# Block-sparse attention of an eight-core decoder kernel: finer filler, early masks added in PSUM, an early gate tile, blocks in another order, shorter waits of the exponentials

## Chip, cores, metric

One Trainium2 chip, all 8 cores, each with two of the 16 sequences and no exchange between them. The metric is device time in microseconds (us) of the slowest core, median of the runs.

## The reference, cut to what matters

```python
for l in range(2):                       # x (16, 2048, 1024)
    h = rms_norm(x, g_pre); proj = h @ w_in          # q/k/v of 16 heads, gate_a, gate_b
    o_a = dilated attention, 3 groups of 4 heads, combined by softmax denominators
    # block-sparse: each query sees its own block of 256 keys and the 3 best-gated past ones
    s = q @ k.T * SCALE - slope * dist; s = where(dist >= 0, s, -inf)    # 4 heads
    o_b = softmax(s) @ v
    merged = sigmoid(gate_a) * (o_a @ W_a) + sigmoid(gate_b) * (o_b @ W_b)
    x = x + rms_norm(merged @ w_out, g_post)
    h = rms_norm(x, g_pre2); u = gelu(conv3(h @ w_gate)) * (h @ w_up)
    x = x + rms_norm(u @ w_down, g_post2)
```

## The kernel before

A core runs four mixers (2 sequences x 2 layers), each followed by its feed-forward part. The normed, transposed activations `hT` (bf16, 8 chunks of 128 rows x 2048 tokens) stay in SBUF; weights come through a ring of 8 slabs, loaded by GpSimd's queue (`Stream`, L303). `Q` (L29) puts every engine's program in the order in which Python emits it, with semaphore waits; each engine is in order. The emission order is made by generators that yield costs in us: `merge(main, fill, ratio)` (L83) gives the filler `ratio` times the cost of what the main generator has yielded, `par` (L119) runs several side by side, `chain` one after the other.

A mixer has three parts:

- Six dilated units (`dil_unit`, L660), with projections of the next unit as filler (`proj_fm`, L621: four groups of eight 512-column products, 1.75 us each, for tokens 0-511, ...). GpSimd adds the units' results (L748) from `tz` buffers that ScalarE fills (L372).
- The block-sparse part (`moba`, L876). Its units are (block, kt, h): a block `(qg, pair)` is 512 queries of one pair of heads; kt runs over the 4*qg+4 tiles of 128 keys, h over the two heads: 160 units in the order of `blocks` (L877), of which 8 of each block touch the diagonal. Unit n issues the scores S (L943, up to 512 columns, into banks 0 to 2), the exponential on ScalarE into `Pm` (L951), on the diagonal a multiplication with the 0/1 triangle `tri` on VectorE (L955), and then, four units behind (`SKEW`), the product with V (L656) into bank 3 or 4. At a block's end VectorE copies both heads' sums out (L972), and a chain of small DMAs over DRAM takes their denominators to 128 partitions, where VectorE inverts them (L908), and back (`norm_den`, `norm_recip`, `bcast`), until `norm_mult` (L900) writes `obT`. `todo` starts these steps after counts of units, so that no queue should wait. The filler `fill_m` (L1113) runs, side by side, the last q projection followed by the top-3 selection of pair 1 (`gating`, L821: tiny products L837, MAX8 L848, transposes L866), the same selection of pair 0, and the denominators of the dilated heads (`dil_den`, L755, ends with four multiplications L785 of 64x1024); it then waits for the first four blocks to be `done` and goes on with the gates of the first 1024 tokens.
- `gates` (L983): per 128 output columns and 512 tokens two gate projections with Tanh (L1001, L1007) and two branch products (`wbr`) multiplied in on VectorE (L1013 to L1022); then `tail_out` (products L538) beside the gates of the other half.

The exponentials (L949) wait on `waits`, here `m_wait` (L1096), which holds the last GpSimd additions of the dilated units (`st["u_last"]`).

Of the kernel before, what the change touches and what calls it, by code (L numbers as in the profile page):

```python
# [8 lines left out]
BF16 = mybir.dt.bfloat16  # L9
AF = mybir.ActivationFunctionType  # L10
ALU = mybir.AluOpType
# [71 lines left out]
def merge(main, fill, ratio):  # L83
    credit = 0.0
    live = fill is not None
    for cost in main:
        credit += cost * ratio
        while live and credit > 0:
            try:
                credit -= next(fill)  # L90
            except StopIteration:
                live = False
    if live:
        for _ in fill:
            pass

# [39 lines left out]
def build(n_seq=2, n_layers=2):  # L136
# [16 lines left out]
    tri_d = dt_in("tri", [128, 128], BF16)  # L153
    qaug_d = dt_in("qaug_t", [4, 64, SEQ], BF16)
# [9 lines left out]
    with es:  # L164
# [24 lines left out]
        tri = sb("tri", [128, 128], BF16)  # L189
        pastc = sb("pastc", [128, 3, 128], F32)  # L190
# [381 lines left out]
        AB = [carve((12 + 2 * i) * KB, 512) for i in range(4)]  # L572
        uT = carve(0, 11264, BF16).rearrange("p (c t) -> p c t", c=NFC)
# [302 lines left out]
        def moba(qk_toks, aug_toks, sel_toks, vm_toks, done, waits, on_p0):  # L876
            blocks = [(0, 0), (1, 0), (0, 1), (1, 1), (2, 0), (2, 1), (3, 0), (3, 1)]  # L877
# [27 lines left out]
            def norm_recip(k, qg, pair, tl):  # L905
# [11 lines left out]
                todo.append([16 if k < 4 else 28, lambda: norm_mult(k, qg, pair, rt)])  # L917
                todo.append([6 if k < 4 else 10, bcast])

            def norm_den(k, qg, pair, te):  # L920
# [8 lines left out]
                todo.append([6 if k < 4 else 10, gather])  # L929
                todo.append([16 if k < 4 else 24, lambda: norm_recip(k, qg, pair, tl)])  # L930

            for n in range(len(units) + SKEW):
                if n < len(units):
# [9 lines left out]
                    tS = PE.do(nc.tensor.matmul(ps[bS][:, 0:nq], lhsT=Kx[:, kt * 128:(kt + 1) * 128],  # L943
                                                rhs=Qx[:, qg * 512 + c0:(qg + 1) * 512], start=True, stop=True))
# [4 lines left out]
                    ACT.wait(tS, pfree[sl], waits)  # L949
# [33 lines left out]
        def gates(l, hf, oa_toks, ob_done, banks, waits, toks, wload):  # L983
            abf = st.setdefault("ab_free", [[], [], [], []])
            mT = mTs[hf]
            for oc in range(8):
                bga, tga, sga = load_w(l, 24 + oc)
                bgb, tgb, sgb = load_w(l, 32 + oc)
                bwa, twa, swa = wbr_ring.load((l, oc, 0))
                bwm, twm, swm = wbr_ring.load((l, oc, 1))  # L990
                tp = None
                for tgi in range(2):
                    tg = 2 * hf + tgi
                    tsl = slice(tg * 512, (tg + 1) * 512)
                    ia = tgi * 2
                    A_, B_ = AB[ia], AB[ia + 1]
                    b_ga = banks.get()
                    t_ga = mm_group(ps[b_ga], [(bga[:, kc * 128:(kc + 1) * 128], hT[:, kc, tsl]) for kc in range(8)],
                                    [tga, hT_tok[4 * tg:4 * tg + 4]])
                    ACT.wait(t_ga, abf[ia], waits)  # L1000
                    s1 = ACT.do(nc.scalar.activation(out=A_, in_=ps[b_ga], func=AF.Tanh, scale=0.5))  # L1001
                    bank_free[b_ga] = [s1]
                    yield 1.75
                    b_gb = banks.get()
                    t_gb = mm_group(ps[b_gb], [(bgb[:, kc * 128:(kc + 1) * 128], hT[:, kc, tsl]) for kc in range(8)], [tgb])
                    ACT.wait(t_gb, abf[ia + 1])
                    s2 = ACT.do(nc.scalar.activation(out=B_, in_=ps[b_gb], func=AF.Tanh, scale=0.5))  # L1007
                    bank_free[b_gb] = [s2]
                    yield 1.75
                    b_ya = banks.get()  # L1010
                    t_ya = mm_group(ps[b_ya], [(bwa[:, kc * 128:(kc + 1) * 128], oaT[:, kc, tsl]) for kc in range(2)], [twa, oa_toks])
                    DVE.wait(s1, t_ya)
                    m1 = DVE.do(nc.vector.scalar_tensor_tensor(out=A_, in0=A_, scalar=1.0, in1=ps[b_ya], op0=ALU.add, op1=ALU.mult))  # L1013
                    bank_free[b_ya] = [m1]
                    b_yb = banks.get()
                    t_yb = mm_group(ps[b_yb], [(bwm[:, kc * 128:(kc + 1) * 128], obT[:, kc, tsl]) for kc in range(2)], [twm, ob_done(tg)])
                    tp = t_yb
                    DVE.wait(s2, t_yb)
                    m2 = DVE.do(nc.vector.scalar_tensor_tensor(out=B_, in0=B_, scalar=1.0, in1=ps[b_yb], op0=ALU.add, op1=ALU.mult))
                    bank_free[b_yb] = [m2]  # L1020
                    DVE.wait(m1, m2, waits)
                    m3 = DVE.do(nc.vector.tensor_tensor(out=mT[:, oc, tgi * 512:(tgi + 1) * 512], in0=A_, in1=B_, op=ALU.add))  # L1022
                    abf[ia] = [m3]
                    abf[ia + 1] = [m3]
                    toks.append(m3)
                    wload()
                    yield 0.9
                slab_ring.release(sga, tp)
                slab_ring.release(sgb, tp)
                wbr_ring.release(swa, tp)  # L1030
                wbr_ring.release(swm, tp)
# [5 lines left out]
        def mixer(s, l, xs_tok, p_wait, pre):  # L1037
# [15 lines left out]
            for i, (g, sp) in enumerate(order):  # L1053
# [36 lines left out]
                merge(dil_unit(g, sp, QK[i % 2], qt[(g, sp)], vt[g], acc_free, res), fill, max(total, 20.0 if i == 3 else 0.0) / 6.9)  # L1090
# [22 lines left out]
            def fill_m():  # L1113
                yield from par(chain(mqk_proj(l, 1, 0, w1, mq[1], FB2), gating(1, mq[1], aug_t[1], sel[1], FB2)),
                               gating(0, mq[0], aug_t[0], sel[0], FB2), dil_den(1, m_wait, nt1))
                while not all((q, p) in done for q in range(2) for p in range(2)):
                    yield 0.5
                yield from gates(l, 0, nt1, ob_done, FB2, nt1, mts, wout_load)
            merge(moba(mq, aug_t, sel, vt[3], done, m_wait, on_p0), fill_m(), 1.25)
# [323 lines left out]
```

How the kernel before makes its waits and increments, by code:

```python
    def wait(self, *toks):  # L49
        acc = {}
        self._collect(toks, acc)
        for so, v in acc.items():
            if self.seen.get(so, 0) >= v:
                continue
            self.seen[so] = v
            if self.pending is not None:
                self.eng.wait_ge(self.pending[0].sem, self.pending[1])
                self.pending = None
            if self.attach:
                self.pending = (so, v)
            else:
                self.eng.wait_ge(so.sem, v)
# [1 line left out]
    def flush(self):  # L64
        if self.pending is not None:
            self.eng.wait_ge(self.pending[0].sem, self.pending[1])
            self.pending = None
# [1 line left out]
    def do(self, inst):  # L69
        if self.pending is not None:
            inst._wait_ge(self.pending[0].sem, self.pending[1])
            self.pending = None
        inst.then_inc(self.so.sem, 1)
        self.so.n += 1
        return (self.so, self.so.n)
# [98 lines left out]
        def dma_tr(out, in_, so):  # L174
            nc.sync.dma_start_transpose(out=out, in_=in_).then_inc(so.sem, 16)
            so.n += 16
            return (so, so.n)
# [1 line left out]
        def dma(q, out, in_, so, **kw):  # L179
            q.eng.dma_start(out=out, in_=in_, **kw).then_inc(so.sem, 16)
            so.n += 16
            return (so, so.n)
```

## Time and profile before

| | |
|---|---|
| median of 3 runs | 3836.77 us (3836.76 to 4285.7) |
| profiled execution, own time | 3838.05 us |
| its span (first to last instruction, slowest core) | 3836.7 us |
| spans of the 8 cores | 3830.6 to 3836.7 us |
| block-sparse parts (first to last S) | from 257 to 387, 1198 to 1331, 2142 to 2273, 3088 to 3220 us |

The time and the span of the profiled execution lie 1.35 us apart. "Busy" adds up instructions; a wait is put down to what released it last. A TensorE row is drawn with its whole latency: the next product may start before it ends.

### The profile page before, as it was taken

To read this page: it belongs to the slowest core of one execution; us is meant where nothing else is said; L and a number is where in the kernel's file an instruction comes from. 1 tells how busy PE (TensorE), PEld (TensorE's weight loads), DVE (VectorE), ACT (ScalarE), POOL (GpSimd) and SP (SyncE) were. 2 spreads that over 40 slices of the span, in tenths; PEclk is the share of its full clock that TensorE was granted. 3 is DMA by queue.
4 is the path that set the end of the run, shared out by engine and by line. 5 is a ranking of instruction groups with operands and counts; after the bars stand their busy time and mean duration, and the time that the engine had idled before them with its cause. 6 is when DMAs were issued, how large, how long until landed. Compare 5 with 4: busy or idle time off the path is not lost.

```text
span 3836.7 us, 55540 instructions; the slowest of 8 cores (3830.6 to 3836.7 us)
## 1 busy us (share of the span) xinstructions
PE 3721.5 (97%) x19760; PEld 1803.8 (47%) x19760; DVE 2033.1 (53%) x3113; ACT 1743.5 (45%) x3389; POOL 875.8 (23%) x1484
## 2 busy tenths in 40 slices
PE   6999999999998999999999899999999989999999
PEld 4644444444564444444465344444446534444444
DVE  4364666464346466646434646754643464675463
ACT  2456345254245635535334653543533464364351
POOL 2331332111133133211113223321111322331110
PEclk8999999999999999999999999999999999999999
DMA  6143788454323379865543257884542325796341
GB/s 149 29 78 56 155 173 168 113 99 90 82 34 70 64 164 181 148 161 90 118 97 54 49 90 167 172 144 127 77 103 54 55 51 101 159 191 120 105 71 72
DMA packets 303863, 410.32 MB, mean 107 GB/s; under 512 B 150560, under 2 KB 167200, under 8 KB 303584
## 3 DMA queue, kind: packets, MB, share of 16 engines
q0 software_dynamic: 118656, 190.89, 32.5%
q1 hardware_dynamic: 184944, 215.88, 20.2%
q8 instruction: 170, 2.79, 0.3%
q14 instruction: 93, 0.76, 0.1%
HBM read 500.52 MB, written 67.63 MB: 148 GB/s over the span
## 4 chain that ended last, share of the span: by engine, by line
PE 92%; DVE 3%; ACT 2%; POOL 1%; DMA 1%; issue 1%; SPq 0%; POOLq 0%; DVEq 0%; ACTq 0%
PE psum L383 57%; PE psum L1250 16%; PE psum L538 6%; PE psum L606 5%; PE psum L656 5%; PE psum L943 3%; PE psum L687 1%; ACT s_arena L951 1%; DVE s_arena L785 0%; POOL s_xr L748 0%; DMA s_xr<-x 0%; ACT s_hb L451 0%; DVE s_hb L460 0%; DVE s_arena L900 0%; DMA s_slabs<-w_in_r 0%
## 5 line engine op out<-in xcount | busy, mean ns | idle before, releaser
L383 PE MATMUL psum<-s_hT,s_slabs 128*128 128x512 bf16 x9728 | 2166.4, 379 | 9.6 <-DVE s_arena L1211 2.6
L383 PEld LDWEIGHTS psum<-s_hT,s_slabs 128*128 128x128 bf16 x9728 | 942.9, 98 | 1131.3 <-issue 30.3
L1250 PE MATMUL psum<-s_arena 128*128 128x512 bf16 x2816 | 609.1, 379 | 0.0
L1200 DVE SCALAR_TENSOR_TENSOR s_arena<-s_arena,s_convw 128x512 f32<-128x512 f32 x352 | 264.2, 751 | 425.8 <-ACT s_arena L1192 425.7
L1250 PEld LDWEIGHTS psum<-s_arena 128*128 128x128 bf16 x2816 | 275.6, 98 | 332.2
L420 DVE SCALAR_TENSOR_TENSOR s_tz<-psum,s_stat,s_gpost 128x1024 f32<-128x1024 f32 x128 | 164.1, 1282 | 381.7 <-POOL s_stat L399 381.7
L411 ACT ACTIVATE s_hb<-psum 128x1024 bf16<-128x1024 f32 x128 | 130.9, 1023 | 504.8 <-PE psum L1250 344.8
L656 PE MATMUL psum<-s_arena 128*128 128x128 bf16 (+2 forms) x1840 | 316.6, 267 | 37.4 <-DVE s_arena L955 21.9
L180 POOL DMA_DIRECT2D s_slabs<-w_in_r x224 | 122.4, 550 | 906.6 <-PE psum L656 425.7
L951 ACT ACTIVATE s_arena<-psum 128x512 bf16<-128x512 f32 (+3 forms) x640 | 295.6, 550 | 73.4 <-PE psum L943 59.4
L1191 ACT COPY s_arena<-psum 128x512 f32<-128x512 f32 x352 | 204.9, 582 | 204.5 <-PE psum L383 204.3
L396 POOL TENSOR_SCALAR s_stat<-s_stat 128x1 f32<-128x1 f32 x256 | 61.4, 240 | 1022.8 <-ACT s_hb L411 575.9
L1192 ACT ACTIVATE s_arena<-psum,s_convw 128x512 f32<-128x512 f32 x352 | 275.7, 783 | 0.0
L1203 DVE SCALAR_TENSOR_TENSOR s_arena<-s_arena,s_convw 128x512 f32<-128x512 f32 x352 | 264.7, 752 | 12.5
L180 POOL DMA_DIRECT2D s_slabs<-w_gate_r x176 | 97.5, 554 | 752.6 <-PE psum L383 750.7
L451 ACT ACTIVATE s_hb<-s_xr 128x1024 bf16<-128x1024 f32 x128 | 135.2, 1056 | 291.8 <-DVE s_xr L426 239.7
L460 DVE SCALAR_TENSOR_TENSOR s_hb<-s_xr,s_stat,s_gpre 128x1024 bf16<-128x1024 f32 x128 | 164.3, 1284 | 178.2 <-POOL s_stat L399 167.2
L606 PE MATMUL psum<-s_slabs,s_hT 128*128 128x256 bf16 x2048 | 248.2, 277 | 10.1 <-DVE s_arena L375 9.4
L1211 DVE TENSOR_TENSOR s_arena<-s_arena,psum 128x512 bf16<-128x512 f32 x352 | 239.5, 680 | 3.6 <-ACT s_arena L1209 3.6
L702 DVE TENSOR_TENSOR s_arena<-s_arena,s_dmask 128x512 bf16<-128x512 bf16 (+2 forms) x232 | 143.1, 631 | 183.5 <-ACT s_arena L696 182.3
L696 ACT ACTIVATE s_arena<-psum 128x512 bf16<-128x512 f32 (+2 forms) x232 | 163.2, 721 | 160.2 <-PE psum L687 160.2
L943 PE MATMUL psum<-s_arena 128*128 128x512 bf16 (+3 forms) x640 | 223.1, 357 | 11.5 <-ACT s_arena L951 9.4
(71 smaller groups left out, 3231.5 us busy)
## 6 DMA issues: line engine op xcount, KB each, us to landing
s_slabs<-w_in_r POOLq DMA_DIRECT2D x224, 256.0 KB, 5.1
xs<-s_xr SPq DMA_DIRECT2D x96, 512.0 KB, 3.2
s_xr<-xs SPq DMA_DIRECT2D x96, 512.0 KB, 5.2
s_slabs<-w_gate_r POOLq DMA_DIRECT2D x176, 256.0 KB, 4.5
s_slabs<-w_up_r POOLq DMA_DIRECT2D x176, 256.0 KB, 5.3
s_xr<-x SPq DMA_DIRECT2D x64, 512.0 KB, 6.2
s_arena<-w_down POOLq DMA_DIRECT2D x88, 256.0 KB, 6.7
y<-s_xr SPq DMA_DIRECT2D x32, 512.0 KB, 3.0
```

Source lines behind the costliest of these rows:

```text
L180: q.eng.dma_start(out=out, in_=in_, **kw).then_inc(so.sem, 16)
L383: inst = nc.tensor.matmul(out, lhsT=l_, rhs=r_, start=(i == 0), stop=(i == n - 1))
L538: inst = nc.tensor.matmul(ps[zb + n], lhsT=mT[:, kc, i * 128:(i + 1) * 128], rhs=wout_t[:, kc, n * 512:(n + 1) * 512], start=(kc == 0), st ...
L606: inst = nc.tensor.matmul(ps[b][:, 0:256], lhsT=hT[:, kc, start:start + 127 * d + 1:d], rhs=rhs, start=(kc == 0), stop=(kc == 7))
L656: return nc.tensor.matmul(out, lhsT=V[:, tile, VOFF[hd]:VOFF[hd] + 128], rhs=rhs, start=start, stop=stop)
L943: tS = PE.do(nc.tensor.matmul(ps[bS][:, 0:nq], lhsT=Kx[:, kt * 128:(kt + 1) * 128], rhs=Qx[:, qg * 512 + c0:(qg + 1) * 512], start=True, s ...
L951: tE = ACT.do(nc.scalar.activation(out=Pm[sl][:, 0:nq], in_=ps[bS][:, 0:nq], func=AF.Exp))
L1192: tt1 = ACT.do(nc.scalar.activation(out=t1_, in_=ps[b_a], func=AF.Identity, bias=convw[:, l, fc, 3:4], scale=convw[:, l, fc, 2:3]))
L1200: d1 = DVE.do(nc.vector.scalar_tensor_tensor(out=t1_, in0=a_[:, 1 + 512 * tgi:513 + 512 * tgi], scalar=convw[:, l, fc, 1:2], in1=t1_, op0= ...
L1203: d2 = DVE.do(nc.vector.scalar_tensor_tensor(out=t1_, in0=a_[:, 512 * tgi:512 + 512 * tgi], scalar=convw[:, l, fc, 0:1], in1=t1_, op0=ALU. ...
L1211: u1 = DVE.do(nc.vector.tensor_tensor(out=uT[:, u["fc"], u["tsl"]], in0=u["t1"], in1=ps[u["b_u"]], op=ALU.mult))
L1250: inst = nc.tensor.matmul(ps[zb + n], lhsT=uT[:, kc, i * 128:(i + 1) * 128], rhs=wdn[kc][:, n * 512:(n + 1) * 512], start=(kc == 0), stop= ...
```

## The change

1. `proj_fm` and the gate projections yield after four of their eight products too, so filler comes in halves of 0.87 us.
2. The two blocks of queries 0-1023 (`qg < 2`) get the causal mask on TensorE: a second product of `identb` with `ntri` (-30000 above the diagonal) is added to the first 128 columns of S. Their 32 multiplications on VectorE per mixer are gone. `ntri` is one more constant, loaded once.
3. The gate projections of the first tile (oc 0) run before the first four blocks are done, in `AB0` buffers of their own, with costs scaled by 3.4, so that they are spread; its branch products follow when all four are done. Slabs are released one by one at their last projection.
4. `blocks` puts (3, 0) before (2, 1).
5. The exponentials wait for `p_free`, the last V product of the dilated units, which read the memory under `Pm`, and no longer for GpSimd's additions.
6. Selection and denominators run as a filler of their own (`side`), pair 1 after a pause of 8; in the first four blocks the inversion comes 11 units after the copy (16), its gather 5 (6), the multiplication 17 after the inversion (16).

```diff
-            blocks = [(0, 0), (1, 0), (0, 1), (1, 1), (2, 0), (2, 1), (3, 0), (3, 1)]
+            blocks = [(0, 0), (1, 0), (0, 1), (1, 1), (2, 0), (3, 0), (2, 1), (3, 1)]
...
-                todo.append([16 if k < 4 else 28, lambda: norm_mult(k, qg, pair, rt)])
+                todo.append([17 if k < 4 else 28, lambda: norm_mult(k, qg, pair, rt)])
...
-                todo.append([6 if k < 4 else 10, gather])
-                todo.append([16 if k < 4 else 24, lambda: norm_recip(k, qg, pair, tl)])
+                todo.append([5 if k < 4 else 10, gather])
+                todo.append([11 if k < 4 else 24, lambda: norm_recip(k, qg, pair, tl)])
...
+                    diag = kt >= 4 * qg
+                    pe_mask = diag and qg < 2
+                    inst = nc.tensor.matmul(ps[bS][:, 0:nq], lhsT=Kx[:, kt * 128:(kt + 1) * 128],
+                                            rhs=Qx[:, qg * 512 + c0:(qg + 1) * 512], start=True, stop=not pe_mask)
+                    if pe_mask:
+                        inst = nc.tensor.matmul(ps[bS][:, 0:128], lhsT=identb[:, :], rhs=ntri[:, :], start=False, stop=True)
...
-                    ACT.wait(tS, pfree[sl], waits)
+                    ACT.wait(tS, pfree[sl], p_free)
...
-                    if kt >= 4 * qg:
+                    if diag and not pe_mask:
...
+            first = 0
+            if early is not None:
+                bufs, e_wait, factor, ready = early
                 for tgi in range(2):
+                    yield from scaled(gate_mm(0, tgi, bufs, e_wait), factor)
+                while not ready():
+                    yield 0.5
+                for tgi in range(2):
+                    yield from branch_mm(0, tgi, bufs)
+                first = 1
+            for oc in range(first, 8):
+                for tgi in range(2):
+                    yield from gate_mm(oc, tgi, AB, waits)
+                    yield from branch_mm(oc, tgi, AB)
...
+            def fill_pe():
+                yield from scaled(mqk_proj(l, 1, 0, w1, mq[1], FB2), 1.5)
+                yield from gates(l, 0, nt1, ob_done, FB2, nt1, mts, wout_load, (AB0, nt0, 3.4, ready))
+            side = par(chain(pause(8.0), gating(1, mq[1], aug_t[1], sel[1], FB2)),
+                       gating(0, mq[0], aug_t[0], sel[0], FB2), dil_den(1, m_wait, nt1))
+            merge(moba(mq, aug_t, sel, vt[3], done, ures[(2, 1)]["pv_tok"], m_wait, on_p0), (side, 1.25), (fill_pe(), 1.25))
```

`gate_mm` is the Tanh half of the old loop and `branch_mm` the other; `scaled` multiplies the costs, `pause` yields without work.

TensorE at the start of the first block-sparse part, before: S of the first units (L943), filler (L383), V products (L656).

```order
L943 MATMUL psum<-s_arena 128x512
L383 MATMUL psum<-s_hT,s_slabs 128x512 x8
L943 MATMUL psum<-s_arena 128x512
L943 MATMUL psum<-s_arena 128x384 x2
L383 MATMUL psum<-s_hT,s_slabs 128x512 x8
L943 MATMUL psum<-s_arena 128x256
L656 MATMUL psum<-s_arena 128x512
L943 MATMUL psum<-s_arena 128x256
```

And with the change (S L965, mask L968, filler L643, V product L676):

```order
L965 MATMUL psum<-s_arena 128x512
L968 MATMUL psum<-s_ntri,s_identb 128x128
L643 MATMUL psum<-s_hT,s_slabs 128x512 x4
L965 MATMUL psum<-s_arena 128x512
L968 MATMUL psum<-s_ntri,s_identb 128x128
L965 MATMUL psum<-s_arena 128x384
L968 MATMUL psum<-s_ntri,s_identb 128x128
L643 MATMUL psum<-s_hT,s_slabs 128x512 x4
L965 MATMUL psum<-s_arena 128x384
L968 MATMUL psum<-s_ntri,s_identb 128x128
L965 MATMUL psum<-s_arena 128x256
L968 MATMUL psum<-s_ntri,s_identb 128x128
```

The first eight-product groups are cut in two, and each S is followed by a 128-column mask.

VectorE where the last early blocks and block (2, 0) meet, before: copies L972, dilated multiplications L785, triangle masks L955, multiplications L900, inversions L908.

```order
L972 COPY s_tz<-psum 128x512 [waits q_pe] x2
L785 TENSOR_TENSOR s_arena<-s_xr,s_arena 64x1024 [waits den3]
L785 TENSOR_TENSOR s_arena<-s_xr,s_arena 64x1024
L955 TENSOR_TENSOR s_arena<-s_arena,s_tri 128x128 [waits q_act] x2
L785 TENSOR_TENSOR s_arena<-s_xr,s_arena 64x1024
L955 TENSOR_TENSOR s_arena<-s_arena,s_tri 128x128 [waits q_act]
L900 TENSOR_TENSOR s_arena<-s_arena 64x512 [waits dm03]
L900 TENSOR_TENSOR s_arena<-s_arena 64x512
L908 RECIPROCAL s_cdm<-s_cdm 128x8 [waits dm11]
L955 TENSOR_TENSOR s_arena<-s_arena,s_tri 128x128 [waits q_act]
L785 TENSOR_TENSOR s_arena<-s_xr,s_arena 64x1024
L955 TENSOR_TENSOR s_arena<-s_arena,s_tri 128x128 [waits q_act] x4
```

And with the change (copies L997, dilated multiplications L805, L920, L928, masks L980):

```order
L805 TENSOR_TENSOR s_arena<-s_xr,s_arena 64x1024 [waits den3]
L805 TENSOR_TENSOR s_arena<-s_xr,s_arena 64x1024 x3
L928 RECIPROCAL s_cdm<-s_cdm 128x8 [waits dm21]
L997 COPY s_arena<-psum 128x512 [waits q_pe,q_dve]
L997 COPY s_arena<-psum 128x512 [waits q_pe]
L920 TENSOR_TENSOR s_arena<-s_arena 64x512 [waits dm13]
L920 TENSOR_TENSOR s_arena<-s_arena 64x512
L928 RECIPROCAL s_cdm<-s_cdm 128x8 [waits dm01]
L920 TENSOR_TENSOR s_arena<-s_tz 64x512 [waits dm23]
L920 TENSOR_TENSOR s_arena<-s_tz 64x512
L980 TENSOR_TENSOR s_arena<-s_arena,s_tri 128x128 [waits q_act] x8
L997 COPY s_arena<-psum 128x512 [waits q_pe,q_dve]
```

The dilated multiplications stand in one piece with no mask between or behind them; all eight masks of block (2, 0) come after the multiplications of the early blocks.

TensorE from the last unit of the early blocks into block (2, 0), before, a stretch with no filler:

```order
L943 MATMUL psum<-s_arena 128x512
L656 MATMUL psum<-s_arena 128x128
L943 MATMUL psum<-s_arena 128x512
L656 MATMUL psum<-s_arena 128x128
L943 MATMUL psum<-s_arena 128x512
L656 MATMUL psum<-s_arena 128x512
L943 MATMUL psum<-s_arena 128x512
L656 MATMUL psum<-s_arena 128x512
```

And with the change, where L1025 is half a gate projection of the early tile:

```order
L965 MATMUL psum<-s_arena 128x512
L676 MATMUL psum<-s_arena 128x128
L965 MATMUL psum<-s_arena 128x512
L676 MATMUL psum<-s_arena 128x128
L965 MATMUL psum<-s_arena 128x512
L676 MATMUL psum<-s_arena 128x512
L1025 MATMUL psum<-s_hT,s_slabs 128x512 x4
L965 MATMUL psum<-s_arena 128x512
L676 MATMUL psum<-s_arena 128x512
L965 MATMUL psum<-s_arena 128x512
```

Before, no projection stands among the 73 units 10 to 82; now four halves of the last q projection and the eight of the early tile stand among them, and only the 21 units 58 to 78 have none.

## Rows read from the trace of the kernel before

**Rows 1.** The page: the chain that ended last, by engine
```profile
PE 92%; DVE 3%; ACT 2%; POOL 1%; DMA 1%; issue 1%; SPq 0%; POOLq 0%; DVEq 0%; ACTq 0%
```

**Rows 2.** Busy time by stretch (window: length, busy us and count per engine)
```profile
core 1: us, PE busy (x) PEld busy (x) DVE busy (x) ACT busy (x) POOL busy (x), PEclk, DMA share, GB/s
256.97:312.73 55.76, 44.40 (x257) 19.85 (x258) 34.40 (x121) 38.41 (x87) 5.94 (x7) 0.97 0.25 52
312.73:386.95 74.22, 73.61 (x351) 33.48 (x351) 28.90 (x63) 47.31 (x98) 12.18 (x23) 1.00 0.41 63
386.95:1200.47 813.52, 807.53 (x4312) 394.48 (x4311) 443.52 (x592) 350.75 (x665) 203.69 (x347) 1.00 0.56 113
1200.47:1254.40 53.93, 42.77 (x237) 19.08 (x235) 32.96 (x118) 34.71 (x79) 2.82 (x3) 0.91 0.23 46
...
2141.65:2198.00 56.35, 44.95 (x253) 20.15 (x254) 34.44 (x121) 38.08 (x86) 4.91 (x5) 0.94 0.22 49
...
3088.50:3145.00 56.50, 45.14 (x252) 20.10 (x253) 34.41 (x121) 37.67 (x85) 4.87 (x5) 0.94 0.21 45
```

**Rows 3.** TensorE's waits over the span: total us, times, longest
```profile
PE psum L656 <- DVE s_arena L955: 21.9, 20, 1.4
PE psum L943 <- ACT s_arena L951: 9.4, 12, 2.5
...
PE psum L656 <- DVE s_gsm L848: 4.5, 8, 0.8
PE psum L656 <- DVE s_cdm L908: 4.0, 4, 1.0
...
PE psum L656 <- DVE s_tz L972: 3.1, 8, 0.6
...
PE psum L383 <- ACT s_tz L372: 2.6, 3, 0.9
```

**Rows 4.** TensorE in order of time, first mixer: start, duration, [idle before, releaser]
```profile
262.07 0.32 PE L943 MATMUL psum<-s_arena 128*128 128x384 bf16 x1 [1.57 <-ACT s_arena L951]
...
271.43 0.38 PE L656 MATMUL psum<-s_arena 128*128 128x512 bf16 x1 [0.84 <-DVE s_gsm L848]
...
292.48 0.32 PE L656 MATMUL psum<-s_arena 128*128 128x384 bf16 x1 [0.79 <-DVE s_arena L955]
...
294.12 0.32 PE L656 MATMUL psum<-s_arena 128*128 128x384 bf16 x1 [1.26 <-DVE s_arena L955]
```

**Rows 5.** VectorE in the same stretch
```profile
272.06 0.63 DVE L848 MAX8 s_gsm<-s_gsm 128x8 f32<-128x8 f32 x8
...
280.41 0.69 DVE L972 COPY s_arena<-psum 128x512 f32<-128x512 f32 x1
...
287.65 2.34 DVE L785 TENSOR_TENSOR s_arena<-s_xr,s_arena 64x1024 bf16<-64x1024 f32 x2
```

**Rows 6.** The window behind these waits
```profile
296.00:299.00 3.00, 3.00 (x10) 1.09 (x9) 1.53 (x4) 2.26 (x4) 0.00 (x0) 0.54 0.26 91
```

**Rows 7.** ScalarE at the start of the block-sparse part
```profile
256.91 1.07 ACT L372 COPY s_tz<-psum 128x512 f32<-128x512 f32 x2 [1.01 <-PE psum L656]
...
261.33 0.60 ACT L951 ACTIVATE s_arena<-psum 128x512 bf16<-128x512 f32 x1 [3.35 <-POOL s_xr L748]
```

**Rows 8.** TensorE: four 128-column products, then a projection group
```profile
241.58 0.40 PE L656 MATMUL psum<-s_arena 128*128 128x128 bf16 x4
241.82 1.89 PE L383 MATMUL psum<-s_hT,s_slabs 128*128 128x512 bf16 x8
```

**Rows 9.** The chain that ended last, in order of time
```profile
299.05 6.87 ACT s_arena L951 x14
```

**Rows 10.** SyncE's issues of a block's denominators
```profile
283.09 0.63 SPq L180 DMA_DIRECT2D dm<-s_arena  x2
...
284.98 0.53 SPq L180 DMA_DIRECT2D s_cdm<-dm  x1
```

**Rows 11.** The tile s_cdm in this stretch: its DMAs
```profile
DMA to landing us min/median/max: 1.4/1.6/2.5
```

More of the change, by code:

```diff
@@ L80, with merge, scaled, pause @@
 KB = 256
-def merge(main, fill, ratio):
-    credit = 0.0
-    live = fill is not None
+def merge(main, *fills):
+    live = [[gen, ratio, 0.0] for gen, ratio in fills]
     for cost in main:
[L87 to L94, printed above, removed]
-            pass
+        for f in list(live):
+            f[2] += cost * f[1]
+            while f[2] > 0:
+                try:
+                    f[2] -= next(f[0])
+                except StopIteration:
+                    live.remove(f)
+                    break
+    for f in live:
+        for _ in f[0]:
+            pass
+def scaled(gen, factor):
+    for cost in gen:
+        yield cost * factor
+def pause(cost):
+    for _ in range(int(2 * cost)):
+        yield 0.5
 def chain(*gens):
@@ L572, in build @@
         AB = [carve((12 + 2 * i) * KB, 512) for i in range(4)]
+        AB0 = [carve((60 + 2 * i) * KB, 512) for i in range(4)]
         uT = carve(0, 11264, BF16).rearrange("p (c t) -> p c t", c=NFC)
@@ L981, in moba, with gates @@
                 yield 0.43
-        def gates(l, hf, oa_toks, ob_done, banks, waits, toks, wload):
+        def gates(l, hf, oa_toks, ob_done, banks, waits, toks, wload, early=None):
             abf = st.setdefault("ab_free", [[], [], [], []])
             mT = mTs[hf]
[L986 to L991, printed above, removed]
-                for tgi in range(2):
[L993 to L1031, printed above, removed]
@@ new lines, in gates, with gate_mm @@
+            w = {}
+            def gate_mm(oc, tgi, bufs, waits):
+                tg = 2 * hf + tgi
+                tsl = slice(tg * 512, (tg + 1) * 512)
+                if tgi == 0:
+                    w[oc] = [load_w(l, 24 + oc), load_w(l, 32 + oc)]
+                out = []
+                for j in range(2):
+                    buf, tok, s_ = w[oc][j]
+                    b = banks.get()
+                    PE.wait(tok, hT_tok[4 * tg:4 * tg + 4])
+                    inst = None
+                    for kc in range(8):
+                        inst = nc.tensor.matmul(ps[b], lhsT=buf[:, kc * 128:(kc + 1) * 128], rhs=hT[:, kc, tsl], start=(kc == 0), stop=(kc == 7))
+                        if kc == 3:
+                            yield 0.87
+                    t_g = PE.do(inst)
+                    ACT.wait(t_g, abf[2 * tgi + j], waits)
+                    s1 = ACT.do(nc.scalar.activation(out=bufs[2 * tgi + j], in_=ps[b], func=AF.Tanh, scale=0.5))
+                    bank_free[b] = [s1]
+                    out.append(s1)
+                    if tgi == 1:
+                        slab_ring.release(s_, t_g)
+                    yield 0.87
+                w[(oc, tgi)] = out
@@ L1111, in ob_done, with ready @@
                 return [done[(tg, p)] for p in range(2)]
[L1113 to L1119, printed above, removed]
+            def ready():
+                return len(nt1) == 4 and all((q, p) in done for q in range(2) for p in range(2))
+            def fill_pe():
[4 more added lines that the diff above has]
+            merge(moba(mq, aug_t, sel, vt[3], done, ures[(2, 1)]["pv_tok"], m_wait, on_p0), (side, 1.25), (fill_pe(), 1.25))
             while wq:
@@ L1294, in qk_tg @@
                     next(gen)
+                    next(gen)
                 yield
@@ L1404, in _constants @@
         "tri": tri.astype(bf),
+        "ntri": ((1.0 - tri) * NEG).astype(bf),
         "qaug_t": qaug_b, "kaug_t": kaug_b,
```

51 lines of the change are left out of this document (42 added, 9 removed).

## Prediction

> **What bounds the kernel now.** I read the page first, then busy time by stretch, then TensorE's waits, and last the timeline of the worst stretch. The page shows a kernel that is TensorE from end to end: 92% of the chain that ended last [rows 1]. The stretches then show where the rest lies. Outside the block-sparse parts there is nothing to get: 807.5 busy of 813.5 us between the first and the second one, and the late half of a block-sparse part, where gate projections are filler, is busy 73.6 of 74.2. The early part, some 55 us in each of the four mixers, is not: TensorE idles 11.36, 11.16, 11.40 and 11.36 us there, 45.3 in all, and its granted clock is 0.97, 0.91, 0.94 and 0.94 [rows 2].
>
> The waits say for whom [rows 3]: 21.9 us for the triangle masks on VectorE (L955), 9.4 for exponentials (L951), 4.5 behind the MAX8 of the selection, 4.0 behind an inversion, 3.1 and 2.6 for copies. That is 45.5 us in 55 waits. The masks themselves are short; they stand in VectorE's queue behind longer work. Two dilated multiplications take 2.34 us from 287.65 on [rows 5], and behind them and their successors TensorE starts late three times, by 0.79 and 1.26 us [rows 4] and once more by about 1. The window from 296 to 299 us right behind is granted 0.54 of the clock, which is the 1.2 GHz level most of the time, after these idle pieces; the windows further on are back at 1.00 [rows 6, 2].
>
> Three corrections make these waits a price. A wait is drawn shorter than it is: a 512-column product is drawn with 0.38 us [rows 4], but a group of eight takes 1.89, so the next one can start after (1.89 - 0.38) / 7 = 0.216 [rows 8]. Each wait therefore costs 0.16 us more: 55 x 0.16 = 8.8. The missing clock is 0.03 x 55.8 + 0.09 x 53.9 + 0.06 x 56.4 + 0.06 x 56.5 = 13.3 us of full-speed time. And ScalarE paces TensorE where no filler stands: 14 exponentials in 6.87 us, 0.49 each [rows 9], against two products, 0.43, an excess of 0.06 on some 35 wide units of a mixer: 8.4 in four. Together 45.5 + 8.8 + 13.3 + 8.4 = 76 us, 2.0% of the time. This is all that the change can reach.
>
> **The change part by part**, for all four mixers, against the profiled execution's own 3838.05 us.
>
> *Masks in PSUM.* All but the last of the five waits of a mixer for L955 are in the early blocks, where the exponential's output now goes straight to the V product. The fifth, in block (2, 0), had a pair of L900 between its masks; the new order puts all early multiplications ahead of the eight masks. I let all 20 go: 21.9 + 20 x 0.16 = 25.1. The price: 32 products of 128 columns per mixer, 128 in all. Four such products in a row start within 241.82 - 241.58 = 0.24 us, 0.06 each, with their own weight loads [rows 8]: 7.7 us. The far end is a product that nothing overlaps, 0.40 - 3 x 0.06 = 0.22 us [rows 8]: 28 us. I take 0.06, because the row shows exactly this, two products of 128 columns that add up in one bank between others. The row speaks for 0.06; the Trainium skill, "TensorE: Matmul & The Clock Gate", section "Back-to-back issue gap", gives about 81 ns for each 128-column product in a stream of loads and products. By that rule the masks would cost 10.4 us and the sum would lose 2.7; the trace decides for the row.
>
> *Shorter wait of the exponentials.* The first exponential starts at 261.33 after 3.35 us of waiting for GpSimd, though ScalarE's own copies end at 256.91 + 1.07 = 257.98 [rows 7]. It will start there. The waits at the start go, 1.57 us in the first mixer [rows 4] and up to 2.5 in the others [rows 3], together 7.3 of the 9.4 us for L951; with 4 x 0.16: 7.9. Late next is the bank that the same copies free (L372, 2.6 us): it stays.
>
> *Selection and copies.* VectorE no longer carries 32 masks of a mixer between the MAX8 groups. The two waits for L848 shrink from 1.4 to about 0.4 per mixer, since a block's first V product needs its predecessor's bank: the copy takes 0.69 [rows 5], TensorE has 0.4 to 0.5 us of work meanwhile. 4.2 go. The wait behind L908 goes (4.6), but at the next block's start eight MAX8, 0.63 us [rows 5], now stand between the two copies: copy, MAX8, copy end 2.1 us after the last product, TensorE has 0.8: 1.3 x 4 = 5.2 comes back. Of the waits for `tz` (3.1 + 8 x 0.16 = 4.4) 2.8 go behind filler, and 2.0 come at the start of block (2, 0), where the four dilated multiplications, 4.7 us at 2.34 for two [rows 5], now stand in one piece: the work queued there (6.4 us) just fits the 6.4 us of products up to that bank's need. Together 4.2 - 0.6 + 0.8 = 4.4.
>
> *Finer filler and the early tile.* These move TensorE's work and add none. Twelve halves of 0.86 us into units 10 to 57 give ScalarE its 0.06 per unit back; 21 units, mostly wide, stay bare. Of 8.4 us I let 4 go. The early tile's four Tanh are pieces like an exponential, 0.60 us [rows 7], for a ScalarE that was busy 38.4 of 55.8 us [rows 2]: hidden. With the three late starts gone the clock should hold; I take 80% of 13.3, 10.6. In the dilated units pairs of groups of 16 and 8 become 12 and 12; a few bank waits go there, 1.5 us from a total of some 5 for copies.
>
> *Earlier inversion.* At 11 units the gather must have landed. The path is: issue of the two copies at 283.09, gather issued at 284.98, landed 1.6 later, 3.5 us [rows 10, 11]. Eleven units are at least 11 x 0.43 = 4.7 us, plus two halves of filler, 6.4. It costs nothing; without that margin VectorE would stand, and with it the next block's copies. The order of blocks only puts selection 1 further from its use.
>
> Sum: 25.1 + 7.9 + 4.4 + 4 + 10.6 + 1.5 = 53.5 saved, 7.7 paid, net 45.8: 3838.05 - 45.8 = 3792.3. The median of the runs is 1.3 below that execution, so 3791.
>
> **The rivals.** *The waits come back in another place.* VectorE stays in order, its four dilated multiplications are one block of 4.7 us just ahead of a bank's copy with no slack left by my own count, and the eight masks of (2, 0) follow two more pairs. If half of the masks' 25.1 reappears as waits for copies, and the clock falls as before, 12.5 + 10.6 us are missing: 3814. For it: the slack of zero. Against it: the projections between units are not counted in that slack on the side of the blocks after it.
>
> *More goes than I count.* If the bank waits at block starts hide behind the halves, 5.2 + 2.0 + 1.6 us, and ScalarE's pace too, 4.4, it is 13 us less: 3778.
>
> *Masks at their far end.* 128 x 0.22 = 28 instead of 7.7: 3811. For it: each mask needs `identb` loaded between two loads of other weights. Against it: rows 8.
>
> *Slower: VectorE waits for the gather.* The inversion at 11 units stands in front of everything in VectorE's queue. In 16 early blocks the price is what the gather lands later than 6.4 us after the copy. It eats the gain from 6.4 + 45.8 / 16 = 9.3 us on; at 10.5 us the time is 3838 - 45.8 + 16 x 4.1 = 3858. For it: SyncE's queue is in order and holds the other chain's DMAs too. Against it: 3.5 us in the rows, a factor of 2.6 away.
>
> **How the numbers follow.** Forecast 0.52, waits come back 0.20, more goes 0.15, masks dear 0.10, slower 0.03. The range leaves out the slow rival and the tails of the others: 3773 to 3818. A measurement of this kernel tells some 2% from no change, 77 us; that is below 3760, and all waits, pace and clock together (76) less the masks (7.7) end at 3770. So faster by over 2% is 0.03, within 2% is 0.95, slower by over 2% (beyond 3914) 0.02.
>
> **What would show it.** Right: in the early stretch of each mixer TensorE idles 2 to 4 us instead of 11, nothing waits for the triangle masks, the first exponential starts within 0.2 us of the last `tz` copy, the clock is 0.98 or more, masks start 0.06 us after their S has streamed, and the first to last S of a mixer take about 119 us instead of 130. Wrong: waits for L997 or L928 of over 1 us in several blocks; idle DMA waits before L928; a mask's start over 0.1 us after its time; or a gain in the time that lies outside these four stretches.

## The result and the profile after

| | before | changed |
|---|---|---|
| median | 3837.59 us | 3795.72 us (3794.95 to 4152.6, 4 runs) |
| ratio | | 0.9887, interval [0.9873, 0.9902] |
| slowest core's span | 3836.7 us | 3793.6 us |
| granted clock of the cores | 0.992 to 0.994 | 0.996 to 0.998 |

The change saves 42 us, 1.1%: within 2%, as forecast, and 4.7 us above the predicted 3791. Both medians are of one comparison, which leaves disturbed runs (as the one at 4152.6) out of its ratio; below, the time given of each run is the median of its undisturbed executions.

The page of the changed kernel: busy time, and the chain by engine, which was 92% TensorE [rows 1].

```profile
PE 3708.5 (98%) x19888; PEld 1806.4 (48%) x19888; DVE 2008.8 (53%) x2985; ACT 1756.4 (46%) x3389; POOL 876.3 (23%) x1484
...
PE 94%; DVE 3%; ACT 1%; issue 1%; DMA 1%; POOL 0%; SPq 0%; DVEq 0%; POOLq 0%; ACTq 0%
```

Busy time by stretch of the changed kernel, on core 7: the early part of each mixer, and the late part of the first (columns as in [rows 2], which they answer).

```profile
256.45:310.00 53.55, 50.76 (x321) 24.41 (x322) 31.97 (x91) 40.32 (x90) 9.18 (x12) 1.00 0.35 67
310.00:383.90 73.90, 73.47 (x356) 34.21 (x355) 28.93 (x65) 50.23 (x99) 13.74 (x26) 1.00 0.47 71
1189.30:1243.00 53.70, 51.50 (x324) 24.65 (x324) 31.97 (x91) 41.04 (x91) 7.00 (x8) 1.00 0.30 62
2120.50:2174.20 53.70, 51.77 (x326) 25.02 (x327) 33.21 (x93) 41.40 (x91) 7.07 (x8) 1.00 0.32 62
3056.70:3110.40 53.70, 50.96 (x321) 24.44 (x322) 32.16 (x92) 40.46 (x90) 7.02 (x8) 1.00 0.30 62
```

The idle time of the four stretches is 53.55 - 50.76 = 2.79, 2.20, 1.93 and 2.74 us, 9.7 in all where 45.3 stood, and the clock is 1.00 in each. The late part is as it was. The instruction counts differ because the early tile and the masks now lie in the stretch: in the first mixer it holds 64 more TensorE instructions in 2.2 us less.

TensorE's waits over the span of the changed kernel (S L965, V product L676, filler L643, tail products L551):

```profile
PE psum L643 <- DVE s_km L833: 4.6, 9, 0.6
PE psum L551 <- DVE s_arena L1056: 4.0, 4, 1.0
...
PE psum L676 <- DVE s_arena L997: 2.4, 4, 0.6
PE psum L676 <- DVE s_gsm L868: 1.8, 4, 0.5
...
PE psum L676 <- DVE s_cdm L928: 1.7, 4, 0.4
PE psum L643 <- ACT s_tz L385: 1.7, 2, 0.9
...
PE psum L965 <- ACT s_arena L976: 1.4, 4, 0.3
```

Against [rows 3]: the 21.9 us for the triangle masks are gone altogether, the exponentials' 9.4 are 1.4, the selection's 4.5 are 1.8 (four waits of at most 0.5), the inversions' 4.0 are 1.7. Two are new. L551, the first product of `tail_out`, waits 1.0 us in each mixer for the last addition of the branch products (L1056). L643 <- L833 is a filler projection that waits for a bank which VectorE still reads for the key means; it takes the place of another wait of the dilated units.

ScalarE, then TensorE, at the start of the first block-sparse part of the changed kernel:

```profile
256.43 1.07 ACT L385 COPY s_tz<-psum 128x512 f32<-128x512 f32 x2 [0.27 <-PE psum L676]
257.38 0.62 ACT L976 ACTIVATE s_arena<-psum 128x512 bf16<-128x512 f32 x1
```

```profile
256.66 0.22 PE L968 MATMUL psum<-s_ntri,s_identb 128*128 128x128 bf16 x1
257.75 1.02 PE L643 MATMUL psum<-s_hT,s_slabs 128*128 128x512 bf16 x4 [0.87 <-ACT s_tz L385]
258.61 0.38 PE L965 MATMUL psum<-s_arena 128*128 128x512 bf16 x1
258.83 0.22 PE L968 MATMUL psum<-s_ntri,s_identb 128*128 128x128 bf16 x1
258.88 0.33 PE L965 MATMUL psum<-s_arena 128*128 128x384 bf16 x1
```

The first exponential starts at 257.38, right behind the copies, where it stood idle for 3.35 us [rows 7]. A mask is drawn with 0.22 us but takes the line for little of it: S at 258.61, its mask at 258.83, the next S at 258.88. That is 0.05 us between mask and next S. The 0.87 us wait for the bank is the one that the prediction let stand.

### The profile page after: what moved, and what is told of

Read it like the earlier page. It is cut to its first block, busy times and chain, and to the rows that moved or that the text cites. A ratio compares the mean times of both kernels' runs of the same rounds, so it can differ in the third digit from the quotient of the medians.

```text
span 3793.6 us, 55772 instructions; the slowest of 8 cores (3790.2 to 3793.6 us)
## 1 busy us (share of the span) xinstructions
PE 3708.5 (98%) x19888; PEld 1806.4 (48%) x19888; DVE 2008.8 (53%) x2985; ACT 1756.4 (46%) x3389; POOL 876.3 (23%) x1484
## 4 chain that ended last, share of the span: by engine, by line
PE 94%; DVE 3%; ACT 1%; issue 1%; DMA 1%; POOL 0%; SPq 0%; DVEq 0%; POOLq 0%; ACTq 0%
PE psum L396 35%; PE psum L1297 16%; PE psum L1025 12%; PE psum L643 11%; PE psum L551 6%; PE psum L676 5%; PE psum L620 5%; PE psum L965 3%; PE psum L707 1%; DVE s_arena L722 0%; DMA s_xr<-x 0%; ACT s_arena L716 0%; DVE s_arena L388 0%; DVE s_arena L997 0%; DVE s_hb L473 0%
## 5 line engine op out<-in xcount | busy, mean ns | idle before, releaser
L1025 PE MATMUL psum<-s_hT,s_slabs 128*128 128x512 bf16 x2048 | 489.7, 379 | 0.4
L643 PE MATMUL psum<-s_hT,s_slabs 128*128 128x512 bf16 x2048 | 473.1, 379 | 12.0 <-DVE s_km L833 4.6
L976 ACT ACTIVATE s_arena<-psum 128x512 bf16<-128x512 f32 (+3 forms) x640 | 306.3, 542 | 86.3 <-PE psum L965 63.2
L676 PE MATMUL psum<-s_arena 128*128 128x128 bf16 (+2 forms) x1840 | 314.7, 264 | 7.6 <-DVE s_arena L997 2.4
L1025 PEld LDWEIGHTS psum<-s_hT,s_slabs 128*128 128x128 bf16 x2048 | 198.2, 98 | 232.7 <-issue 7.1
L643 PEld LDWEIGHTS psum<-s_hT,s_slabs 128*128 128x128 bf16 x2048 | 191.5, 98 | 226.2 <-issue 24.5
```

The lines of the kernel that those rows point to most:

```text
L643: inst = nc.tensor.matmul(ps[b], lhsT=buf[:, kc * 128:(kc + 1) * 128], rhs=hT[:, kc, tg * 512:(tg + 1) * 512], start=(kc == 0), stop=(kc = ...
L676: return nc.tensor.matmul(out, lhsT=V[:, tile, VOFF[hd]:VOFF[hd] + 128], rhs=rhs, start=start, stop=stop)
L976: tE = ACT.do(nc.scalar.activation(out=Pm[sl][:, 0:nq], in_=ps[bS][:, 0:nq], func=AF.Exp))
L1025: inst = nc.tensor.matmul(ps[b], lhsT=buf[:, kc * 128:(kc + 1) * 128], rhs=hT[:, kc, tsl], start=(kc == 0), stop=(kc == 7))
```

## The experiments

Most are the changed kernel (3795.7) with one edit; three, which say so, start from the kernel before. In 23 of the 25 executions counted beside them the kernel before lies between 3836.2 and 3840.3 (the other two are 3844.8 and 3875.7), so 3837.6 is used for it.

**Masks back on VectorE.**

```diff
-                    pe_mask = diag and qg < 2
+                    pe_mask = False
```

> The changed kernel with one part undone: the diagonal masks of the early blocks are VectorE multiplications again (pe_mask = False), everything else as changed. Theory A (VectorE's queue: the masks stood behind longer work, and the clock fell after the late starts): most of the waits for the masks come back, of 25.1 us some 15 because the filler halves now lie between, the clock gives back up to 8, and 7.7 us of mask products go: 3795.7 + 15 = about 3811 us. Theory B (the evenly spread filler is what helps, the place of the masks does not matter): the 128 mask products go and nothing comes back, about 3788 us.

Measured: 3813.5, ratio to the kernel before 0.9931 [0.9907, 0.9955]. That is 17.8 more than the changed kernel: A. TensorE's waits now hold again

```profile
PE psum L676 <- DVE s_arena L980: 10.8, 16, 1.7
...
PE psum L676 <- DVE s_gsm L868: 5.8, 8, 1.0
```

10.8 for the masks, 4.0 more behind the selection, and the clock of the cores is 0.995 to 0.997. In the first 58 us of the early stretches the clock is 1.00, 0.94, 1.00 and 0.97, some 5 us of full-speed time lost. So the 17.8 hold waits and clock, less the masks' own price.

**Masks in PSUM alone, on the kernel before.** The same edit the other way round: the second product, `ntri`, and no multiplication for `qg < 2`.

> The kernel before with this part alone: early diagonal masks added in PSUM, filler, order, waits and delays as before. Theory A: sixteen of the twenty waits for the masks go (20 us), with them most of the lost clock (8 us), 7.7 us of products come: about 3837 - 20 = 3817 us, TensorE's waits for the masks at 4 us or less. Theory B: the filler gap of 73 units and ScalarE's pace are as before, so the waits turn into waits for exponentials and copies: 3837 + 0 to 7 = about 3840 us.

Measured: 3820.6 (two executions, 3820.3 and 3820.8), 17.0 less than before: A by the time. The masks in PSUM have a worth of their own, the same at either end. The waits behind VectorE do not all go with them:

```profile
PE psum L658 <- DVE s_arena L979: 9.3, 12, 1.2
PE psum L947 <- ACT s_arena L958: 9.0, 12, 2.4
PE psum L658 <- DVE s_arena L962: 5.4, 4, 2.4
```

L962 are the masks of block (2, 0), 5.4 us in four waits, and the copies of the block sums (L979) now make TensorE wait 9.3. So "the waits come back in another place" is what this edit does alone. What it brings besides is clock. The first 58 us of each mixer's block-sparse part, TensorE alone:

```profile
255.30:313.30 58.00, 48.57 (x303) 0.97 0.24 50
1195.60:1253.60 58.00, 49.89 (x314) 1.00 0.21 48
2132.00:2190.00 58.00, 49.59 (x314) 1.00 0.22 48
3074.60:3132.60 58.00, 49.92 (x315) 1.00 0.23 48
```

TensorE idles 34.0 us there; in windows of the same length the kernel before idles 45.5, at 0.97, 0.91, 0.94 and 0.94. So 11.5 us are idle time and some 12 are clock (13.9 lost before, 1.7 now), less the price of the masks.

**Each mask issued twice.** It adds the mask a second time: 128 more products, the masked scores are -60000 instead of -30000.

> The changed kernel with each early mask product issued twice (the second adds another -30000 where one already stands, nothing is left out): 128 more products of 128 columns, to price one in place. At 0.06 us each: 3795.7 + 7.7 = 3803.4 us. By the rule of the Trainium skill, page TensorE: Matmul & The Clock Gate, section Back-to-back issue gap, at about 81 ns each: 3806.1 us. At the far end of the prediction, 0.22 us each: 3824 us.

Measured: 3801.7, from 3798.7 to 3801.8 in three executions: 3.0 to 6.1 us more, 0.02 to 0.05 us per mask, below the 0.06 taken. Each doubled mask has its own weight load (20016 loads against 19888), though of the same weights as the mask ahead of it. The 0.05 us between mask and next S, above, are of the masks as they stand in the kernel. The two dearer prices are out.

**The exponentials' old wait.**

```diff
-                    ACT.wait(tS, pfree[sl], p_free)
+                    ACT.wait(tS, pfree[sl], waits)
```

> The changed kernel, but the exponentials wait for GpSimd's last additions again. Theory A: the start waits of 1.6 to 2.5 us per mixer come back, 7.9 us in all: about 3803.5 us, and the first exponential starts some 3.4 us after ScalarE's last copy. Rival: the finer filler covers it in part, since four halves stand among the first eight units, or the whole early stretch catches up: 3797 us.

Measured: 3813.7, ratio 0.9930 [0.9907, 0.9952]: 18 more, twice A's price. The waits, and three windows at the start of the second mixer's block-sparse part (TensorE alone):

```profile
PE psum L965 <- ACT s_arena L976: 13.1, 8, 3.6
```

```profile
1190.00:1200.00 10.00, 6.03 (x41) 1.00 0.20 28
1200.00:1210.00 10.00, 9.31 (x57) 0.83 0.01 2
1210.00:1220.00 10.00, 10.00 (x86) 1.00 0.53 106
```

The wait is dearer than in the kernel before, 13.1 against 9.4. TensorE stands at the fourth S, which needs the bank of the first. In the first mixer it gets there 3.7 us behind the first S, no sooner than before (3.5), but the first exponential starts 5.49 us behind that S instead of 4.36:

```profile
262.44 1.47 ACT L976 ACTIVATE s_arena<-psum 128x512 bf16<-128x512 f32 x3 [4.44 <-POOL s_xr L768]
```

ScalarE is idle for 4.44 us there, where it was 3.35 [rows 7]. Behind the wait, in three of the four mixers, stands a stretch of 10 to 15 us at a clock of 0.83 to 0.89, 1.7 us each. 11.7 us of waits and 5 of clock are 16.8 of the 18.

**The exponentials' wait alone, on the kernel before.**

> The kernel before with one edit: the exponentials of the block-sparse part wait only for the last V product of the dilated units. Undoing this in the changed kernel cost 18 us: 11.7 of waits and a clock of 0.83 for 10 us behind the wait in three mixers (some 5). Theory A (the edit has a price of its own, the prediction's): in the kernel before the wait costs 7.9 us and the clock was low behind it in one mixer (0.83 for 10 us, 1.7), so 3837.6 - 9.6 = 3828. Rival B (before, the wait hides another one, VectorE's queue with its masks and selection, which then ends last): less than 4 us, 3834 to 3838.

Measured: 3830.8, ratio 0.9966 [0.9936, 0.9996]: 7 less, between the two, and near the prediction's 7.9 for the waits. TensorE's waits for exponentials fall from 9.4 to 2.1. The clock of the cores stays at 0.992 to 0.994 there, and the early stretches stay at 0.97, 0.94, 0.94 and 0.93.

**Masks and the wait, on the kernel before.**

> The kernel before with two edits: the early masks in PSUM (alone 3820.5) and the shorter wait of the exponentials. Theory A (the edits add up): 3820.5 less what the shorter wait gives alone, 3811 by the prediction's price. Theory B (they help each other, because the clock stays up once both idle places are gone): 3805 or less. Either way what is left down to 3795.7 of the changed kernel is what finer and spread filler gives.

Measured: 3813.8 (3812.1, 3813.8 and 3826.1), ratio 0.9951 [0.9929, 0.9973]: A, the sum of the two edits, 17.0 and 6.8, is 3813.8 too. The first 58 us of the early stretches are idle for 26.1 us in all. What is left down to 3795.7, 18 us, is a remainder and not a run of its own: finer and spread filler, the early tile, `side` and the counts of units together. In the changed kernel the same windows are idle for 9.7.

**No early tile.** All gate projections start when four blocks are done.

```diff
+                while not ready():
+                    yield 0.5
-                yield from gates(l, 0, nt1, ob_done, FB2, nt1, mts, wout_load, (AB0, nt0, 3.4, ready))
+                yield from gates(l, 0, nt1, ob_done, FB2, nt1, mts, wout_load)
```

> The changed kernel without the early tile: its eight halves per mixer come only when the first four blocks are done, 58 units without a projection. Theory A: only ScalarE's pace and the block starts suffer, 4 us of pace and 2 to 4 of waits for copies in all: about 3802 us. Theory B (spread filler is the gain): over 20 us come back, 3815 us or more, with the clock under 0.95 in the early stretches.

Measured: 3819.8 (seven executions from 3816.6 to 3821.5, and one at 3848.7), ratio 0.9957 [0.9932, 0.9982]: 24 more, and A falls. On core 6 the waits show why, and VectorE's rows, then TensorE's, of the first mixer:

```profile
PE psum L676 <- DVE s_arena L997: 15.6, 8, 4.1
```

```profile
283.66 0.20 DVE L928 RECIPROCAL s_cdm<-s_cdm 128x8 f32<-128x8 f32 x1 [1.71 <-DMA s_cdm<-dm]
...
285.16 4.74 DVE L805 TENSOR_TENSOR s_arena<-s_xr,s_arena 64x1024 bf16<-64x1024 f32 x4
289.94 0.20 DVE L928 RECIPROCAL s_cdm<-s_cdm 128x8 f32<-128x8 f32 x1
290.06 1.24 DVE L997 COPY s_arena<-psum 128x512 f32<-128x512 f32 x2
```

```profile
290.84 0.59 PE L676 MATMUL psum<-s_arena 128*128 128x512 bf16 x1 [3.08 <-DVE s_arena L997]
```

The four dilated multiplications are one block of 4.74 us. With no projections beside it TensorE is through with the block's products before VectorE comes to the copies at 290.06, and the first V product of the next block waits 3.08 us for them. The block itself starts late: the inversion ahead of it stands 1.71 us for its gather. In the four mixers TensorE waits 3.08, 4.09, 2.23 and 3.85 us here, and the inversion ahead of the block 1.71, 2.71, 0.85 and 2.48. The difference is 1.37 or 1.38 each time, so 7.75 of these 13.25 us hang on the gather and 5.5 on the block. In the changed kernel the same inversion waits for nothing, and the copies wait for TensorE:

```profile
286.97 0.18 DVE L928 RECIPROCAL s_cdm<-s_cdm 128x8 f32<-128x8 f32 x1
...
288.46 4.74 DVE L805 TENSOR_TENSOR s_arena<-s_xr,s_arena 64x1024 bf16<-64x1024 f32 x4
...
294.31 1.29 DVE L997 COPY s_arena<-psum 128x512 f32<-128x512 f32 x2 [0.88 <-PE psum L676]
```

Behind the waits the clock is 0.87, 0.86, 0.93 and 0.93 over 25 us, some 10 us of full-speed time. With 13.2 us more of waits for copies (15.6 against 2.4) this is 23.5 of the 24. The place is the one where the prediction had counted 6.4 us of work against 6.4 us of products. Without the tile it falls short by 1.4 and by the gather; with it 0.9 is to spare.

**The old counts of units.**

```diff
-                todo.append([17 if k < 4 else 28, lambda: norm_mult(k, qg, pair, rt)])
+                todo.append([16 if k < 4 else 28, lambda: norm_mult(k, qg, pair, rt)])
...
-                todo.append([5 if k < 4 else 10, gather])
-                todo.append([11 if k < 4 else 24, lambda: norm_recip(k, qg, pair, tl)])
+                todo.append([6 if k < 4 else 10, gather])
+                todo.append([16 if k < 4 else 24, lambda: norm_recip(k, qg, pair, tl)])
```

> The changed kernel with the old counts of units between copy, gather, inversion and multiplication of the first four blocks (6, 16 and 16 instead of 5, 11 and 17). Theory A (the prediction: earlier inversion costs nothing and gives nothing by itself): 3795.7 within 2 us. Rival B (the shorter counts are what keeps the inversions from standing ahead of the copies of the next block): 3800 or more, with waits for L928 or for copies of over 1 us.

Measured: 3805.4 (3805.0 and 3805.9), ratio 0.9914 [0.9891, 0.9938]: 9.7 more. B has the size, at another place than it named. VectorE in block (2, 0) of this kernel:

```profile
307.37 0.23 DVE L980 TENSOR_TENSOR s_arena<-s_arena,s_tri 128x128 bf16<-128x128 bf16 x1 [0.16 <-ACT s_arena L976]
308.99 1.41 DVE L920 TENSOR_TENSOR s_arena<-s_tz 64x512 bf16<-64x512 f32 x2 [1.40 <-DMA s_tz<-dm]
310.43 0.20 DVE L928 RECIPROCAL s_cdm<-s_cdm 128x8 f32<-128x8 f32 x1
310.55 0.71 DVE L980 TENSOR_TENSOR s_arena<-s_arena,s_tri 128x128 bf16<-128x128 bf16 x5
```

After three masks a pair of multiplications stands in the queue whose DMA has not landed; VectorE idles 1.40, works 1.6, and only then come the other five masks. TensorE waits 2.5 us for them (7.7 us in the four mixers), and the clock from 310 to 320 is 0.83, another 1.7 us. With the new counts the pair is through before the first mask. The earlier inversion does give something: it is this fifth wait for masks of each mixer, which the prediction had credited to the order of blocks.

**The old order of blocks.** `(2, 1)` ahead of `(3, 0)`.

> The changed kernel with block (2, 1) ahead of (3, 0) as before. Theory A (the prediction: the order only puts selection 1 further from its use, which was never late): 3795.7 within 2 us. Rival B (the multiplications and selection 1 come due too early for VectorE in the old order): 3800 or more, with waits for L980 or L868 at the start of block (2, 1).

Measured: 3796.0, ratio 0.9891 [0.9874, 0.9908]: A. With the new counts of units the order is worth nothing.

**Whole groups in the dilated units.** `proj_fm` yields after four products only inside the block-sparse part.

> The changed kernel with whole projection groups in the dilated units (as before), halves only in the block-sparse part and the gates. The prediction gave the halves there 1.5 us of gain; the trace of the changed kernel shows new waits of TensorE for the km reduction instead (L833, 4.6 us in 9) where a wait for L702 of 4 us was before. If the halves cost: about 2 us faster, 3793.7. If the prediction's term holds: 1.5 slower, 3797.2.

Measured: 3793.9, ratio 0.9886 [0.9869, 0.9902]: 1.8 less. The halves cost there: the nine waits for L833 go (4.6 us), the four for `u` additions of 1.0 us (L723 here, L702 before) come back (3.9). This kernel, then the kernel before:

```profile
PE psum L677 <- DVE s_arena L723: 3.9, 4, 1.0
```

```profile
PE psum L656 <- DVE s_arena L702: 3.9, 4, 1.0
```

**Tail products later.**

```diff
-(tail_out(0, mts, mk2), 1.6)
+(chain(pause(1.5), tail_out(0, mts, mk2)), 1.6)
```

> The changed kernel with the first output product of the tail one half-group later, by a pause of 1.5 ahead of it. In the changed kernel this product waits 1.0 us in each mixer for the last gate sum (L551 for L1056, 4.0 us), since only half a projection stands ahead of it, a whole one before. If this wait is a loss of its own: 4 x (1.0 + 0.16) less what the kernel before loses there (0.3 each), 3.4 us faster, 3792.3. If it is hidden by another wait in the tail: 3795.7.

Measured: 3792.2, ratio 0.9882 [0.9862, 0.9901]: 3.5 less, and no wait L551 <- L1056 is left. It was a loss of its own, of 0.9 us per mixer.

**A better version.** The last two edits, and the filler of the block-sparse part begins with another bank than the one that ScalarE empties last (`FB2.i = 1`).

> The two edits just named together (whole groups in the dilated units, the tail's first product later) and a third: the first filler of the block-sparse part takes bank 6, not bank 5, which ScalarE's tz copy holds (wait of 0.87 us in some mixers, 1.7 us in 2, and 1.04 us start to start in the first). Gains of 2 + 3.4 + 2 us if they add: about 3788 us. If the start wait only moves to the V product behind it: 3790.

Measured: 3786.3 (3786.15 to 3786.33), ratio 0.9866 [0.985, 0.9882]: 9.4 less than the changed kernel and 51 less than before. It beats both. The first two edits gave 1.8 and 3.5 alone; the third was not run alone, so the 4.1 us left over are put down to it by subtraction. Early stretch of its first mixer, TensorE alone:

```profile
256.30:310.00 53.70, 51.65 (x325) 1.00 0.35 67
```

The 0.87 us for the bank are gone. What idles there now, 2.05 us, is in pieces of at most 0.6.

## Why the prediction was right

**The sum.** Its likeliest case came true: net 45.8 us expected, 42 measured. The idle time of the early stretches fell by 35.6 us and the clock rose to 1.00 in all of them, so the view that it rested on [rows 2] was the right one. The terms are another matter: several are off, in both directions.

**Masks in PSUM: right in direction, and in size by luck.** 25.1 less 7.7, 17.4, were priced, for waits alone and with the clock as a term of its own. The run that adds the masks alone gives 17.0, the one that takes them out 17.8, but both hold clock: with the masks alone idle time falls by 11.5 us, not 25.1, and the clock gives back some 12. Waits for copies (9.3) and the fifth wait of a mixer (5.4), which goes by the counts of units, stand where the masks' waits stood. Each mask costs 0.05 us at most instead of 0.06. The Trainium skill's 81 ns ("TensorE: Matmul & The Clock Gate", "Back-to-back issue gap") would have given 10.4 us for all; the doubled masks show 3.0 to 6.1, so the measurement decides against it.

**Exponentials: right as an edit to the kernel before, half as one of the changed kernel.** 7.9 priced, 7 alone, 18 on top of the rest. What was missing is that in the changed kernel the exponential would come later behind the first S (5.49 us instead of 4.36), and that the clock behind the wait is at stake once the rest of the stretch holds it.

**Finer filler and the early tile: mis-sized.** "These move TensorE's work and add none ... I let 4 go", with 4.4 for selection and copies and 1.5 in the dilated units. The remainder for this group and the counts of units is 18 us; without the early tile alone 24 are lost. What the tile buys is in the main not ScalarE's pace (TensorE waits for exponentials at V products for 1.8 us without it) but time for VectorE: for its 4.7 us block, which the prediction had seen ("just fits") without saying that this hangs on the tile, and for the gather ahead of it.

**Earlier inversion: "It costs nothing" is right as long as the tile is there, that it gives nothing is wrong.** The counts of units are worth 9.7 us. The order of blocks, in turn, gives 0.3. The path of the gather was priced too short, at 3.5 us. For block (1, 1) of the first mixer it is 4.8 in the changed kernel (copies issued at 295.67, gather landed at 300.5). Without the tile it is 6.8 for block (1, 0) (276.86 to 283.66), because SyncE issues that gather only at 281.03, right behind two other DMAs.

**Halves in dilated units: wrong in sign**, +1.5 priced, -1.8 measured. **Not foreseen**: the wait of `tail_out`, 3.5. These two, 6.8 together, are more than the 4.7 us by which the forecast was low.

**Clock: right in direction, low by some 3.** 10.6 priced as 80% of 13.3; all four stretches are at 1.00, so all of it came. It is contained in the differences above and not a term beside them: the masks alone bring nearly all of it, the shorter wait of the exponentials alone none.

The sizes do not add up when undone one by one: 17.8 + 18 + 24 + 9.7 = 70 for a change of 42. Done one by one, masks and shorter wait add (17.0 + 6.8 against 23.8 for both); the 18 us behind them are a remainder and prove nothing. What fits the rows: each edit undone in the dense kernel loses clock anew, some 5, 5, 10 and 2 us, 22 in all, where the kernel before had 13.3 to lose. The shorter wait on the kernel before leaves the clock where it was; other idle places stand in the same stretches there. That the remaining waits overlap in the same way is likely but not shown.

**The announced signs.** Seen: idle 2 to 3 us per early stretch, no wait for early masks, exponential right behind the copies, clock 0.98 or more, mask 0.05 us. Not seen: "the first to last S of a mixer take about 119 us". They take 127 (256.4 to 383.9), because the early tile's halves, 8 x 0.86 = 6.9, and the masks, 1.9, now lie inside. The sign was badly chosen, not the step. Of the signs against it one is there, "idle DMA waits before L928": VectorE stands 3.60 us for a gather in block (2, 0),

```profile
300.51 0.20 DVE L928 RECIPROCAL s_cdm<-s_cdm 128x8 f32<-128x8 f32 x1 [3.60 <-DMA s_cdm<-dm]
300.63 1.35 DVE L920 TENSOR_TENSOR s_arena<-s_tz 64x512 bf16<-64x512 f32 x2
303.50 0.23 DVE L980 TENSOR_TENSOR s_arena<-s_arena,s_tri 128x128 bf16<-128x128 bf16 x1 [1.52 <-ACT s_arena L976]
```

but nothing is queued behind it that is due: VectorE is through 1.52 us before the first mask.

**The rivals.** "The waits come back" holds for the masks alone in its waits (9.3 us at the copies; idle time falls by half of what was priced), not in its clock, and is prevented by the filler and the tile. "Masks dear" is out by the doubled masks. "VectorE waits for the gather" did not come in the changed kernel, where earlier inversion helps, but it is real without the tile: 7.75 us of TensorE's waits. "More goes" did not come; 3.5 and 1.8 of it were there to be had, as the better version shows.

## What to carry to other kernels

Price the parts of a bundle both from the kernel before and from the end: what an edit is worth alone can be less than half of what its loss costs later (7 against 18 us here). Where a long piece stands in an in-order queue ahead of a bank's copy, count which filler covers it, add the DMA that the queue waits for ahead of it, and name the cover as the thing that carries the gain. And where a predicted size comes out, look whether it came from the term that was priced. Counts of units that start a step decide what stands ahead of what, so a step moved earlier is worth as much as the queue behind it, not as its own duration.

## What the runs showed of the hardware

A 128-column product accumulated into a bank behind another cost 0.02 to 0.05 us of the time with its own weight load: 128 of them 3.0 to 6.1 us. In the trace the next product starts 0.05 us behind it.

In the changed kernel with the old wait of the exponentials the clock fell behind idle places, but not behind each: in the second mixer TensorE was busy 6.03 of 10 us, the next 10 us were granted 0.83, part of them at the 1.2 GHz level, and those behind 1.00 again; in the first mixer, after a wait of 2.55 us, it stayed at 1.00. In the changed kernel, with no wait over 0.9 us in the early stretches, it was 1.00 in all four. With TensorE busy for 98% of the span the clock of the eight cores was 0.996 to 0.998 over the whole profiled run.
